# Last attention: queries split two heads at a time between its units; latent attention: the output projection's first slabs split inside its loop

## The reference

```python
# even layer, latent attention (8 heads, 128 latent features, 32 rotary)
sc = einsum('bqhc,bkc->bhqk', q_lat, c_kv) + einsum('bqhr,bkr->bhqk', q_rope, k_rope)
p = softmax(sc * scale);  o = einsum('bhqk,bkc->bqhc', p, c_kv)
...                                     # and a neighbourhood attention (8 heads)
o_lat = concatenate([o_mla, o_na]) @ w_out

# odd layer, windowed attention (16 query heads, 2 key heads, one sink per head)
p = softmax(concatenate([sink, q @ kc, where(band_ok, q @ kb, -1e30)]))
o = p[..., 1:1 + n_ctx] @ vc + p[..., 1 + n_ctx:] @ vb
h = h + gate * (o @ w_out)
```

## Time and profile before

| | us |
|---|---|
| median of 3 runs (3253.55 to 3275.64) | 3253.82 |
| profiled execution, its own time | 3257.04 |
| its span | 3254.9 |
| PE busy | 3021.7 (93%) |
| DVE busy | 1639.5 (50%) |
| ACT busy | 1157.7 (36%) |
| latent attention's loop, first score to last exponential | 1611.5 to 1782.9 |
| last attention, first query split | 2644.8 |

### The profile page before, as it was taken

The page is one execution under the profiler, slowest core; times in us unless marked ns, Lnnn a source line. Parts: engine busy times, 40 slices in busy tenths (PEclk is TensorE's granted clock), DMA queues, the critical chain, the costliest instruction groups (busy, mean ns, idle before and its releaser), DMA issues.

```text
span 3254.9 us, 39178 instructions
## 1 busy us (share of the span) xinstructions
PE 3021.7 (93%) x15560; PEld 2527.0 (78%) x15560; DVE 1639.5 (50%) x2759; ACT 1157.7 (36%) x1927; POOL 239.2 (7%) x204
## 2 busy tenths in 40 slices
PE   6899999888888999999798999999999989999998
PEld 4678888565776788878577887888888779878887
DVE  5756666655776667651245754222222545343333
ACT  3532223434663222241345653211112345432222
POOL 2010001000552000010000101000000000000001
PEclk9999999999999999999899999999999989999999
DMA  4235454241002455431000011212111110023232
GB/s 144 72 104 162 154 163 152 68 144 53 1 1 85 137 161 174 141 125 56 33 1 12 30 33 57 67 59 64 61 65 60 62 34 1 21 84 97 92 102 66
DMA packets 75126, 260.08 MB, mean 80 GB/s; under 512 B 8128, under 2 KB 10688, under 8 KB 74816
## 3 DMA queue, kind: packets, MB, share of 16 engines
q1 hardware_dynamic: 74944, 257.57, 24.4%
HBM read 255.44 MB, written 2.10 MB: 79 GB/s over the span
## 4 chain that ended last, share of the span: by engine, by line
PE 76%; DVE 8%; ACT 6%; issue 6%; POOL 3%; DMA 2%; DVEq 0%; SPq 0%; POOLq 0%; ACTq 0%
PE PS L503 74%; POOL PB L1601 2%; PE PS L1249 2%; DVE WL L434 1%; ACT WH L428 1%; DVE SM L2238 1%; DMA RAW<-in_f_in 1%; DMA RAW<-in_kv_v 0%; ACT TMP L1256 0%; DVE TMP L616 0%; PE PS L1283 0%; DMA RAW<-in_a_in 0%; ACT TMP L1240 0%; POOL Q L1609 0%; DVE XR L837 0%
## 5 line engine op out<-in xcount | busy, mean ns | idle before, releaser
L503 PE MATMUL PS<-UH,WH 128*128 128x512 f32 x2296 | 873.1, 380 | 72.3 <-DVE UL L629 19.4
L503 PE MATMUL PS<-UL,WH 128*128 128x512 f32 x2296 | 860.7, 375 | 0.0
L503 PE MATMUL PS<-UH,WL 128*128 128x512 f32 x2296 | 856.2, 373 | 0.0
L428 ACT ACTIVATE WH<-RAW 128x1024 fp32r<-128x1024 f32 (+1 forms) x367 | 379.6, 1037 | 911.4 <-PE PS L503 594.0
L434 DVE TENSOR_TENSOR WL<-RAW,WH 128x1024 fp32r<-128x1024 f32 (+1 forms) x367 | 447.7, 1223 | 380.8 <-ACT WH L428 366.9
L503 PEld LDWEIGHTS PS<-UH,WH 128*128 128x128 f32 x2296 | 440.4, 192 | 166.1 <-DVE WL L434 31.0
L503 PEld LDWEIGHTS PS<-UL,WH 128*128 128x128 f32 x2296 | 440.1, 192 | 79.5 <-issue 6.1
L503 PEld LDWEIGHTS PS<-UH,WL 128*128 128x128 f32 x2296 | 439.1, 191 | 77.5
L503 PE MATMUL PS<-HH,WH 128*128 128x512 f32 x1008 | 368.8, 366 | 2.6 <-DVE HL L2108 2.6
L503 PE MATMUL PS<-HL,WH 128*128 128x512 f32 x1008 | 369.2, 366 | 0.0
L503 PE MATMUL PS<-HH,WL 128*128 128x512 f32 x1008 | 367.4, 364 | 0.0
(11 more groups left out here) (331 smaller groups left out, 4041.6 us busy)
## 6 DMA issues: line engine op xcount, KB each, us to landing
RAW<-in_mod_w SPq DMA_DIRECT2D x96, 512.0 KB, 3.5
RAW<-in_f_in SPq DMA_DIRECT2D x88, 512.0 KB, 3.5
RAW<-in_g_in SPq DMA_DIRECT2D x88, 512.0 KB, 3.4
RAW<-in_f_out SPq DMA_DIRECT2D x32, 448.0 KB, 4.0
RAW<-in_g_out SPq DMA_DIRECT2D x32, 448.0 KB, 3.2
RAW<-in_a_in SPq DMA_DIRECT2D x16, 512.0 KB, 3.6
RAW<-in_f_out SPq DMA_DIRECT2D x16, 512.0 KB, 4.2
RAW<-in_g_out SPq DMA_DIRECT2D x16, 512.0 KB, 3.4
```

What stands on the lines that cost most here:

```text
L428: act.e.activation(hi, raw, ACT.Copy).then_inc(wh.step(n, i), 1)
L503: return pe.e.matmul(out, l, r, start=start, stop=stop)
```

## The change

1. Latent attention. `high(act, "mla_w", 0)` and `low(dve, "mla_w", 0)` leave the preparation and stand in step 9 of the loop, ahead of the exponential (ACT) and of the maximum (DVE) of unit 8. In their old place stand now the rotary queries of head 0, which came last before.
2. Last attention. The 16 + 16 query splits are no longer made in one piece ahead of the loop. The table load comes first, then the two halves of query tile 0 (heads 0 and 1), and each even step s from 0 to 12 begins with the two halves of tile s/2 + 1.

PE, POOL and SP have the same instructions in the same order.

```diff
@@ even_scalar
             psum.leave(("q_up", m), act_e)
-        high(act, "mla_w", 0)
+        rotary_high(act, 0)
         values_evac(act, 0, 0)
         values_evac(act, 0, 1)
         latent_high(act, 0, 0)
         latent_high(act, 0, 1)
-        rotary_high(act, 0)
@@ even_vector
-        low(dve, "mla_w", 0)
+        rotary_low(dve, 0)
         latent_low(dve, 0, 0)
         latent_low(dve, 0, 1)
-        rotary_low(dve, 0)
@@ mla_scalar
         for s in range(len(QU) + 3):
+            if s == 9:
+                high(act, "mla_w", 0)
@@ mla_vector
         for s in range(len(QU) + 4):
+            if s == 9:
+                low(dve, "mla_w", 0)
@@ swa_scalar and swa_vector
+    def swa_split_scalar(act, i):
+        for j in range(2):
+            query_high(act, "swa", i, j, lambda r: QRAW2[r, i, :].rearrange("p (q n) -> p q n", q=4), lambda r: Q2[r, :, 2 * i + j, :],
+                       [dve_q.after("o", i + 1, "rope"), lin.after("o_in", 9)])
+
+    def swa_split_vector(dve, i):
+        for j in range(2):
+            query_low(dve, "swa", i, j, lambda r: QRAW2[r, i, :].rearrange("p (q n) -> p q n", q=4), lambda r: Q2[r, :, 2 * i + j, :], [])
+
     def swa_scalar(act):
-        split_queries("swa", QRAW2, lambda i: [dve_q.after("o", i + 1, "rope"), lin.after("o_in", 9)], "act", act)
         logexp(act)
+        swa_split_scalar(act, 0)
         for s in range(len(SWA) + 5):
+            if s < 14 and s % 2 == 0:
+                swa_split_scalar(act, s // 2 + 1)
...
     def swa_vector(dve):
-        split_queries("swa", QRAW2, None, "dve", dve)
+        swa_split_vector(dve, 0)
         for s in range(len(SWA) + 4):
+            if s < 14 and s % 2 == 0:
+                swa_split_vector(dve, s // 2 + 1)
```

More of the change, by code:

```diff
@@ L1303, in flipped_lo @@
         return lambda m: Q2[:, q, 8 + m:12 + m, :]
[L1305 to L1314, removed]
     Wave = namedtuple("Wave", "g q rows L tiles first last")
```

## The result

The changed kernel takes 3268.1 us (median of 20 runs, 3262.07 to 3280.76), the kernel before beside it 3255.45 us (20 runs, 3248.66 to 3275.64); the ratio is 1.0033, 95% interval 1.0021 to 1.0045, so about 11 us slower (7 to 15). It is within 1%, but the predicted 3253 us and the upper end of the range, 3260, are both too low. The profiled execution took 3264.99 us, with a span of 3262.9. The page's first line, to be held against the earlier trace rows, shows the same instructions on every engine and TensorE (PE) busy 11 us longer. The mean granted clock of this execution is 0.964 of 2.4 GHz and was 0.968, so the growth goes with the clock.

What follows compares the result with a forecast made beforehand. TensorE, busy for 93% of the span, was taken to bound the kernel. Latent attention -4.5 us and last attention +3.5 made -1.0, so 3253 us against the median 3253.82; range 3245 to 3260 us.

Steps and rivals of the forecast that it cites:

- C: Latent loop, step 9: three slabs ahead of unit 8's exponential and maximum delay it, DMAs costing nothing; +5.7 us.
- F: Last attention: six more steps with two query pieces each, 1.81 us more per step; +10.9 us.
- A: Start of the latent attention: first score comes earlier with the slabs gone from ACT's queue; -9.7 us.
- B: Latent attention behind its first score: clock may stay at 1.00; -3 us, bounds nothing and 5 us gained.
- D: Latent loop behind step 9: TensorE's idle of about 6 us may lower the clock; +2.5 us, bounds 0 and 5.
- E: Start of the last attention: first exponential comes earlier, after the table load and four pieces; -7.2 us.
- Rival 1: Last attention: split steps hold the clock down, costing +8 to +10 us; total 3257 to 3259 us; chance 0.15.
- the sum's 3.5: Last attention's forecast total: -7.2 + 10.9 - 0.2 (slow first turns giving back) = +3.5 us.
- The case "3247 to 3257": Whole kernel: the forecast's own span in us, with both latent clock terms anywhere between their bounds; chance 0.61.

Runs made afterwards that it cites:

- e1: Kernel before with only the latent attention's part of the change, last attention as before; ratio 0.9998 to the kernel before.
- e6: Kernel before with the latent part only, first slab split at the end of the preparation, the other two in step 9; ratio 0.9980 to the kernel before.
- e11: Changed kernel plus 6 and 4 extra matmuls in TensorE's idle times at the last attention's first three tile boundaries; ratio 1.0018 to the kernel before.
- e2: Kernel before with only the last attention's part of the change, latent attention as before; ratio 1.0026 to the kernel before.
- e13: Changed kernel with slabs split after preparation and in steps 5 and 7, query pieces inside waits, extra matmuls at three tile boundaries; ratio 0.9940 to the kernel before.
- e7: e2 plus 18 extra matmuls on TensorE ahead of the last attention's first score; ratio 1.0030 to the kernel before.
- e9: Changed kernel with slabs split after preparation and in steps 5 and 7, query pieces inside waits, 18 extra matmuls before last attention's first score; 0.9957 to kernel before.
- e12: e2 plus extra matmuls: 18 before the first score, 7 ending even steps up to 14, 6 and 4 at three boundaries; ratio 1.0011 to the kernel before.

## Why the prediction was wrong

Forecast was 1 us less than before, measured are 11 us more. By the rows of the two profiled executions the latent part is 5.9 us worse than its sum, and the step that failed is C, with a DMA wait of 4.85 us put at nothing. The last attention is 9.0 us worse. The step that failed there is the clock in and behind F: the sum gave it no price, and it cost 1.5 us in the split steps and some 8 us in the last tile.

- **A held**: -10.6 us (16.64 to 6.00), forecast -9.7.
- **B was too large**: from first score to exponential 7 only 0.8 us was gained (11.45 - 10.64), not 3. The clock fell again, for 10 us (20 before), with PE busy without pause in most of it. In e1, where it was down for only 3 us here, exponential 7 came 1.5 us earlier still, so my 3 us would have needed a clock that does not fall. It lay in its bounds.
- **C failed, and it is the step that turns the latent part.** "The DMAs are hidden: nothing reads those slabs until the projection" was the error: the split reads them, and the next slab cannot be fetched before it. The row was there, 4.96 us of DMA, and I counted it as gained in A without asking what released that DMA. The work itself was right (5.67 us estimated from e6, 5.7 forecast); the wait adds 4.85.
- **D held**: +2.2 us from exponential 8 to 12, forecast +2.5 (in e1, with 17 us at half clock there and not 14, it was +4.5). The four make +1.4 for this place by the rows, and e1 measures -0.7 (-6 to +5), where -4.5 was forecast.
- **E held**: -7.1 us, forecast -7.2. **F held in its price**: 1.70 us per split step at full clock, forecast 1.81.
- **Rival 1 came true and I had given it 0.15.** Of the 34 us between 2656 and 2690 us 18 read 0.50. In the split steps it cost less than that rival said: the sixteenth exponential is 5.0 us late, 1.5 more than the sum's 3.5, because at half clock a pair takes 6.7 to 7.1 us against 6.0. My argument against it, that the clock rises once PE is busy without pause, is contradicted by the window from 2658 to 2674 us: 16.00 of 16.00 us busy, and 0.50. The Trainium skill ("TensorE: Matmul & The Clock Gate", A second HAM failure mode) reports of another kernel that short idles between its groups of matmuls make the clock swing. e11, where filling them kept it up across the boundaries, agrees; the changed kernel's first boundary, where 1.50 and 0.75 us of idle left it at 1.00, shows that they do not always.
- **The last tile was in no case.** Some 8 of the 12.5 us that the profiled execution loses in this attention are its second stretch at half clock. A turn there takes 3.54 us and not 2.15; two exponentials in a row:

```profile
2796.36 0.69 ACT L1240 ACTIVATE PB<-PS,SM 128x513 f32<-128x513 f32 x1 [0.83 <-DVE SM L2242]
...
2799.90 0.69 ACT L1240 ACTIVATE PB<-PS,SM 128x513 f32<-128x513 f32 x1 [0.83 <-DVE SM L2242]
```

I had read the clock only around the two places that the change touches. The kernel before has a fall at the same boundary, and a row on it would have shown that the loop has falls of its own, far from the edit.

- **Two slips in the arithmetic.** The case "3247 to 3257" takes the -1.0 us off twice; with its own bounds it is 3248 to 3258. And "less than 1% can't be told from no change" was too coarse: the 20 executions of each kernel tell 0.33% with an interval of 0.24%.

Together by the rows: +1.4 and +12.5, where the two profiled spans differ by 8.0 us. The rest lies outside both places: the changed kernel's profiled execution is 2.95 us earlier already at the last query copy (1591.86 against 1594.81), ahead of anything that the change touches, and gains another 1.3 us between the two attentions and 1.6 behind the last flipped copy.

## What to carry to other kernels

Before work is moved off a critical path, ask of each wait in it what released it. If a load was waiting for this very work, the wait moves with it; split the first of such a row early and the rest once they have landed. In a chain between engines a piece is free only inside the wait of its own engine, behind the instruction that the other engine needs: the same pieces cost 8.5 us in front of the sink copy and the maximum and gained 8 behind them. And where a kernel has falls of the clock of its own, read the granted clock over the whole loop, not at the edit alone, and compare its mean over many executions: one profile of e2 lost 4 us in this loop where its runs lost 8.5.

## What the hardware showed that I had not expected

TensorE, busy 12.00 of 12.00 us, stayed at 1.2 GHz (2802 to 2814 us, and 24 us in all); with the same turns and idle times ahead of it another execution was back at 2.4 GHz after 3 us. The same idle of 1.50 us at a tile boundary was followed by a fall at one boundary and not at another in one and the same execution. Filling the boundaries' idle moved the last copy earlier (7 us in e11, 5 us in e13). Filling the idle ahead of the loop did not (e7, e9, e12): the clock fell later, in e9 for 20.5 us at the third boundary, and in e12 the filling in the split steps ran at half clock in front of work that was waited for.
